# A ninth weight place beside an eight-place ring: filled four times, or once

## The reference, cut to what matters

```python
u = rmsnorm(x, g_mix); z = u @ w_in            # 1024 x 4096: two branches and two gates
ya = rg_lru(causal_conv(xa));  yb = pool_mix(xb)
x = x + (sigmoid(ga) * (ya @ w_proj_a) + sigmoid(gb) * (yb @ w_proj_b)) @ w_out
t = rmsnorm(x, g_moe)                          # mixture of experts, top 4 of 32
for e in range(32):
    gu = t @ w_gate_up[e] + b_gate_up[e]       # w_gate_up[e]: 1024 x 2048, 8 MiB
    gate = min(gu[:, :1024], 7);  up = clip(gu[:, 1024:], -7, 7)
    h = (up + 1) * gate * sigmoid(1.702 * gate)
    out += comb[:, e] * (h @ w_down[e] + b_down[e])   # w_down[e]: 1024 x 1024, 4 MiB
x = x + out
x = x + rmsnorm(p @ w_ple, g_post) * sigmoid(rmsnorm(x, g_ple) @ w_ple_gate)
y = rmsnorm(x, g_final)
```

## Time and profile before

| | us |
|---|---|
| median of 3 runs | 1209.77 (1209.13 to 1209.91) |
| the profiled execution, its own time | 1210.05 |
| its span in the profile | 1208.3 |
| PE busy | 1169.4 (97%) |
| DVE busy | 331.4 (27%) |
| ACT busy | 213.7 (18%) |
| POOL busy | 29.2 (2%) |
| SP's transfers (queue q1) | 440.04 MB, 87.8% of 16 DMA engines' span |

### The profile page before, as it was taken

How to read it: one execution, slowest core, us unless ns; L and a number is a source line. 1 busy time by engine, 2 the same in 40 slices (tenths; PEclk the granted TensorE clock), 3 DMA queues, 4 the chain that set the end, 5 groups by cost and what they waited for, 6 DMA issues and landing times.

```text
span 1208.3 us, 14638 instructions
## 1 busy us (share of the span) xinstructions
PE 1169.4 (97%) x5836; PEld 553.0 (46%) x5836; DVE 331.4 (27%) x864; ACT 213.7 (18%) x420; POOL 29.2 (2%) x64
## 2 busy tenths in 40 slices
PE   9999999999999999999989899999998999799997
PEld 7777777443443434343333333434434343334344
DVE  4844214250322222131312120313222212111223
ACT  2556302112010101101010112120101010101034
POOL 2001000000000000000000020000000000000000
PEclk9999999999999999999999999999999999999999
DMA  9935573679999999999999999999999999999961
GB/s 287 360 141 203 173 279 133 237 283 429 427 428 426 427 426 428 427 427 429 427 428 428 427 428 425 429 427 426 430 426 428 427 428 430 425 428 428 426 260 40
DMA packets 53287, 446.82 MB, mean 370 GB/s; under 512 B 8174, under 2 KB 11470, under 8 KB 28424
## 3 DMA queue, kind: packets, MB, share of 16 engines
q1 hardware_dynamic: 50512, 440.04, 87.8%
q0 software_dynamic: 2464, 5.71, 1.6%
q10 hardware_dynamic: 256, 0.30, 0.1%
HBM read 444.51 MB, written 1.88 MB: 369 GB/s over the span
## 4 chain that ended last, share of the span: by engine, by line
PE 78%; DMA 20%; ACT 1%; DVE 1%; issue 1%; SPq 0%; DVEq 0%
PE ps L1201 31%; PE ps L864 16%; DMA ring<-in_w_gate_up 14%; PE ps L1222 11%; PE ps L1236 4%; PE ps L1083 3%; DMA ring<-in_w_down 3%; DMA ring<-in_w_ple_gate 2%; PE ps L1016 2%; PE ps L1355 2%; PE ps L1178 2%; PE ps L1168 1%; PE ps L898 1%; PE ps L858 1%; PE ps L885 1%; PE ps L1076 1%
## 5 line engine op out<-in xcount | busy, mean ns | idle before, releaser
L1201 PE MATMUL ps<-ring,work 128*64 128x512 f32 x2000 | 443.6, 597 | 2.8 <-DMA ring<-in_w_gate_up 2.6
L1201 PEld LDWEIGHTS ps<-ring,work 128*64 128x64 f32 x2000 | 141.2, 138 | 273.6 <-issue 261.9
L1222 PE MATMUL ps<-ring,work 128*64 128x512 f32 x992 | 223.4, 595 | 19.4 <-DMA ring<-in_w_down 19.4
L864 PE MATMUL ps<-work,ring 128*128 128x288 f32 x736 | 180.6, 407 | 0.0
L864 PEld LDWEIGHTS ps<-work,ring 128*128 128x128 f32 x736 | 139.7, 190 | 39.6 <-issue 1.7
L1222 PEld LDWEIGHTS ps<-ring,work 128*64 128x64 f32 x992 | 70.6, 137 | 146.8 <-issue 127.6
L2122 DVE TENSOR_SCALAR work<-ps 128x512 f32<-128x512 f32 x32 | 22.1, 691 | 374.5 <-PE ps L1201 374.5
L2094 DVE TENSOR_TENSOR work<-ps,gain_pairs 128x256 f32<-128x256 f32 x60 | 25.5, 424 | 286.2 <-PE ps L1083 286.2
L1626 ACT ACTIVATE work<-work 128x512 f32<-128x512 f32 x32 | 20.2, 631 | 442.9 <-DVE work L2122 442.9
L1083 PE MATMUL ps<-work,x_tok 128*128 128x128 f32 x512 | 65.4, 285 | 0.0
L1083 PEld LDWEIGHTS ps<-work,x_tok 128*128 128x128 f32 x512 | 61.8, 197 | 3.9 <-issue 2.0
(11 more groups left out here) (286 smaller groups left out, 663.0 us busy)
## 6 DMA issues: line engine op xcount, KB each, us to landing
ring<-in_w_gate_up SPq DMA_DIRECT2D x125, 2048.0 KB, 29.5
ring<-in_w_down SPq DMA_DIRECT2D x61, 2048.0 KB, 29.6
ring<-in_w_in SPq DMA_DIRECT2D x7, 2048.0 KB, 19.0
work<-in_w_gate_up SPq DMA_DIRECT2D x3, 1536.0 KB, 12.9
ring<-in_w_proj_b SPq DMA_DIRECT2D x2, 2048.0 KB, 10.0
ring<-in_w_proj_a SPq DMA_DIRECT2D x2, 2048.0 KB, 10.1
ring<-in_w_out SPq DMA_DIRECT2D x2, 2048.0 KB, 9.4
ring<-in_w_ple_gate SPq DMA_DIRECT2D x4, 1024.0 KB, 28.6
```

The costliest lines, as they stand in the source:

```text
L864: mm = pe.matmul(out(b), lhs, rhs, start=(k == 0), stop=(k == len(pairs) - 1))
L1201: mm = pe.matmul(ps[half(g), b, :], xg[:, k, i % 2, :], blocks[2 * (k % 2) + at][:, 512 * g:512 * g + 512], start=False, stop=(k == KC - 1))
L1222: mm = pe.matmul(ps[half(g), b, :], hT_of[i % 2][:, 4 * j + k, :], blocks[k][:, 512 * g:512 * g + 512], start=False, stop=(4 * j + k == KC ...
```

## The change

`AHEAD` loses the pieces 18, 27 and 36: place 1 is filled once, with piece 9. Those three pieces go into the ring in one transfer each, and POOL no longer waits for piece 36 before it loads `p_sample`.

```diff
 OPENING = 2
-AHEAD = {8: 0, 9: 1, 18: 1, 27: 1, 36: 1}
+AHEAD = {8: 0, 9: 1}
 EXTRAS = len(AHEAD)
...
             chunk_filled(pool, "out", 0, 0)
             pool.dma_start(g_post_row, g_ple_post[0:1, :]).then_inc(g_post_landed, 16)
-            quads, at = divmod(max(AHEAD), QUAD_PIECES)
-            i, q = STREAM[at]
-            pool.wait_ge(piece_used_up[q], 4 * quads + i + 1)
             pool.dma_start(p_sample_tok, p_sample[0].rearrange("b t d -> (b t) d")).then_inc(p_landed, 16)
```

## The result

The changed kernel takes 1210.98 us (median of 20 runs, 1210.38 to 1214.67) against 1209.30 of the kernel before (20 runs, 1208.69 to 1210.09): ratio 1.0015, 95% interval 1.0008 to 1.0022. That is +1.7 us, slower by less than 0.2%, where 1211.0 us and +1.2 us were forecast. Its profiled execution took 1211.3 us, with a span of 1209.6 (before: 1210.05 and 1208.3).

A forecast was written before the change was run, and what follows sets the result against it. The prediction took the DMA transfer queue, full from 270 us to its last landing, as the bound. 1209.77 us, plus 1.4 for one gap, less 0.2 for unsplit pieces, gave 1211.0 us, range 1209.5 to 1212.8.

The forecast's parts named there:

- The bound: Whole kernel from 270 us: the transfer queue never stops until its last landing at 1168.8 us, which sets the end.
- The place: Ahead of piece 20, issued at 309.3 us: the queue runs dry once, costing 1.4 us.
- PE feels nothing before 545 us: PE's timeline: no ring wait before 540 us; it takes up the delay around 554 us, and the end moves.
- POOL's edit: Load of p_sample at about 293.8 us in place of 417.3, both in the full queue: worth nothing.
- three pieces in one transfer each: Pieces 18, 27 and 36, unsplit: 0.07 us gained for each, 0.2 us in all, bounds 0 and 0.3.
- The gap at 309.3 us: Issue of piece 20: 6.4 us left where 7.8 are needed, so the DMA queue idles 1.4 us.
- the issue ahead of it: Issue of piece 18 at 297.2 us: 8.8 us left, so the queue stays full and nothing is lost.
- where 7.8 us or more is left, the queue stays full: Test for each later issue, from an idle queue's issue-to-landing time of 7.8 us; any shortfall is idle DMA queue.
- The rival that asked for 8.9 us: Queue properly dry at 309.3 and 297.2 us: a start of 8.9 us costs +2.4, giving 1212.2 us; chance 0.17.
- The further 0.6 us of that rival: Same place: 0.6 us more if the 16 engines get out of step, giving 1212.8 us; within that rival's 0.17.

The follow-up runs named there:

- e12_late40: Kernel before, with pieces 40 to 47 each waiting one use longer before issue; 1209.50 us, ratio 0.9999.
- e8_halves_before: Kernel before, with pieces 10 to 13 moved in halves, each first half issued once the half it replaces is used up; 1207.98 us, ratio 0.9987.
- e1_only18: Kernel before, with place 1 filled by pieces 9 and 18 only, 27 and 36 going into the ring; 1209.50 us, ratio 0.9999.
- e2_no18: Kernel before, with place 1 filled by pieces 9, 27 and 36, piece 18 going into the ring; 1211.56 us, ratio 1.0016.
- e3: Kernel before, with piece 21 waiting one use longer before issue; 1210.36 us, ratio 1.0007.
- e4: Kernel before, with piece 21 waiting two uses longer, piece 22 going out later right behind it; 1213.64 us, ratio 1.0033.
- e11: Kernel before, with piece 24 waiting one use longer, for piece 16 in place of 15; 1210.61 us, ratio 1.0010.
- e6_pool_wait: Changed kernel, with POOL again waiting for piece 36 before it loads p_sample; 1210.96 us, ratio 1.0014.
- e9_half20: Changed kernel, with piece 20 alone moved in halves, the first issued once half of piece 12 is used up; 1210.93 us, ratio 1.0012.
- e7_split24: Changed kernel, with pieces 24 to 47 each moved in two transfers, three quarters and one quarter; 1213.10 us, ratio 1.0030.

## Why the prediction was right

**Right.** The bound: the queue of transfers, full from 270 us to the last landing. e12_late40 shows that lateness alone costs nothing, and e8_halves_before that the queue's time counts to the end. The place: one deep dip, ahead of piece 20, because piece 12 is used up 8.6 us after piece 11. e1_only18 and e2_no18 show that the whole loss hangs on where piece 18 lies, and with it on the releases of pieces 18 to 26. That PE feels nothing before 545 us and meets the delay near 554. That POOL's edit is nothing that can be told. That three pieces in one transfer each give back 0.2 us (0.08 each).

**Luck in the total.** 1210.98 us against a forecast of 1211.0 looks like a hit to 0.02 us, and is not. The forecast stood on 1209.77 us for the kernel before, the median of 3 runs; over 20 runs it is 1209.30. The base was 0.5 us too high and the change 0.5 us too small, and the two cancel. What the prediction got right is the mechanism, and the size to within its own range.

**The term that was mis-sized.** The gap at 309.3 us, forecast at 1.4 us, was 1.9 us of lost time, and 2.2 with the issue ahead of it, which was forecast at nothing. The step that failed is the test "where 7.8 us or more is left, the queue stays full". The pairs, with the loss at the issue itself, are: e3 with 7.9 us left and 0.7 lost (1.0 over the 60 us); e4 with 4.5 and 4.0 (4.1); e11 with 7.5 (its expectation) and 1.0 (1.5); and the changed kernel, whose 2.2 us have two parts: at 297 us, with 8.8 left, 0.3 lost (400 GB/s in place of 416 from 295 to 303 us, below), and at 309 us, with 6.4 left, the other 1.9. The expectation of e11 had put these two at 0.1 and 2.1, and the split is no surer than that: with the same issue of piece 18, this window reads 416 in e2_no18 and 410 in e6_pool_wait. For e3 and e4 the undisturbed landing is that of the kernel before, 309.3 + 11.3 = 320.6, less the 0.4 us by which their profiles start later. Time left and time lost add up to 8.3 to 8.6 us in four and to 9.1 us in the fifth, where the prediction had 7.8. The two windows, the kernel before first:
```profile
295.00:303.00 8.00, 8.00 (x58) 3.89 (x55) 0.42 (x1) 2.72 (x4) 0.00 (x0) 1.00 0.98 416
```
```profile
295.00:303.00 8.00, 8.00 (x58) 4.06 (x55) 0.42 (x1) 2.52 (x4) 0.00 (x0) 1.00 0.99 400
```
I had compared an issue-to-landing time in an idle queue with landings in a busy one. The likely reason for the missing 0.7 us is what e4 shows, that much of a transfer is through well before it lands, so that the queue thins out ahead of the landing; no run isolates it. The rival that asked for 8.9 us missed the threshold by less than the 7.8 did, but for another reason, an instruction fetch. One such fetch does stand near 308 to 309 us in all these kernels, so the runs don't exclude that it has a share; but in e11_late24, where the queue was short from 327 us on, there was none from 310 to 335 us. The further 0.6 us of that rival, for engines out of step, had no row behind it.

**Why the sum came out closer than its term.** 2.2 lost, less 0.2 for the unsplit pieces, would be +2.0; measured was +1.7 (interval 1.0 to 2.7). The rate from 350 to 540 us reads 428 GB/s in the changed kernel and 427 in the kernel before: about 0.4 us by these rounded figures, of which two of the three unsplit pieces explain 0.2. The rest is within the noise, and I have no run that separates it. In the other kernels without halved or split pieces, too, the end moves by the lost time less 0.1 to 0.6 us.

## What to carry to other kernels

Where transfers are the bound, cost a later issue by the time that is left until its undisturbed landing, and leave up to one microsecond more than an idle queue's issue-to-landing time (0.5 to 0.8 us more at four places here, 1.3 at a fifth). What was short of it was lost, and well above it an issue cost nothing; e9_half20, with a piece in halves, lost more than this says. Read the loss as missing bytes (GB/s), over a window and then by place, and not off the landings. Of the three later fillings of the extra place here only the one at the thinnest point of the queue paid, so look for the longest pause between two releases near the start.

## What the runs showed of the hardware that was not expected

A landing trails the bulk of its transfer: in e4_late21_by2 the rate was 148 GB/s or less from 313 us on, while the piece in flight landed at 316.3. The queue that ran dry there took 3.3 us from the issue to full rate, by windows of one microsecond. Moving a 2 MiB piece in two transfers cost 0.08 us in a full queue (e7_split24). And the landing of the same issue differed by 2.0 us (9.7 in the changed kernel and 7.7 in e6_pool_wait) though the ends don't differ.
